# Stick-breaking heads of a two-block model: the order of ScalarE's work, of two projections and of a product

## The reference, cut to what matters

```python
hn = rms_norm(h, norm1_g[i])
z = hn @ w_in[i]
qa, ka, va, qb, kb, vb, ob, ib, fb, uc, vc = split_cols(z, IN_SPLITS)
ya = rms_norm(stick_breaking_attention(qa, ka, va), sb_out_g[i])       # 6 heads of 64
qk = jax.nn.silu(causal_depthwise_conv(jnp.concatenate([qb, kb], axis=-1), conv_w[i], conv_b[i]))
hb = mlstm_chunkwise(qb, kb, vb, ib + igate_b[i], fb + fgate_b[i])     # 4 heads of 96
yb = rms_norm(hb, ...) * jax.nn.sigmoid(ob)
yc = rms_norm(spatial_gating(jax.nn.gelu(uc), jax.nn.gelu(vc), ...), sgu_out_g[i])  # 4 groups of 64
h = h + jnp.concatenate([ya, yb, yc], axis=-1) @ w_out[i]
h = h + hierarchical_moe(...)                                          # 32 experts, 2 per token
```

## Time and profile before

| what | value |
|---|---|
| median of 3 runs | 1323.96 us |
| lowest and highest of them | 1319.77, 1328.98 us |
| the profiled execution's own time | 1326.66 us |
| its span, first to last instruction | 1324.9 us |
| mean granted TensorE clock | 0.928 |
| stick-breaking heads in it | 95 to 156 us |
| mLSTM heads and output projection | 156 to 214 us |

### The profile page before, as it was taken

How to read it: one execution, slowest core, us unless ns; L and a number is a source line. 1 busy time by engine, 2 the same in 40 slices (tenths; PEclk the granted TensorE clock), 3 DMA queues, 4 the chain that set the end, 5 groups by cost and what they waited for, 6 DMA issues and landing times.

```text
span 1324.9 us, 21110 instructions
## 1 busy us (share of the span) xinstructions
PE 1147.2 (87%) x7589; PEld 627.8 (47%) x7589; DVE 573.3 (43%) x1638; ACT 244.1 (18%) x510; POOL 34.0 (3%) x174
## 2 busy tenths in 40 slices
PE   6898899995665796999988998997999989979997
PEld 4655555542222345854444445643444534445434
DVE  3552537432222212899775626433233333323334
ACT  2022322110000224001235313111011111111111
POOL 1000100000000000000110001000000000000000
PEclk9898878998778897999999998999899989989989
DMA  9995548689999973354422455679989999999995
GB/s 328 381 343 220 192 155 317 263 346 421 421 420 422 386 240 127 128 190 141 176 90 101 150 193 207 240 302 428 425 335 427 422 414 428 426 414 423 426 406 204
DMA packets 87309, 399.97 MB, mean 302 GB/s; under 512 B 10646, under 2 KB 19352, under 8 KB 58544
## 3 DMA queue, kind: packets, MB, share of 16 engines
q1 hardware_dynamic: 86272, 398.15, 75.8%
q10 hardware_dynamic: 816, 0.52, 0.3%
q0 software_dynamic: 128, 0.03, 0.0%
HBM read 397.60 MB, written 1.07 MB: 301 GB/s over the span
## 4 chain that ended last, share of the span: by engine, by line
PE 46%; DMA 9%; DVE 3%; ACT 1%; SPq 1%; issue 1%; ACTq 1%; DVEq 0%
PE ps L2411 17%; PE ps L468 10%; PE ps L501 7%; DMA big<-in_w_exp_down 7%; PE ps L427 4%; PE ps L440 2%; PE ps L2447 2%; DMA ring<-in_w_exp_gu 2%; SPq L139 1%; SPq L144 1%; PE ps L417 0%; PE ps L487 0%; ACTq L1014 0%; DVE big L2207 0%; DVE big L2205 0%
## 5 line engine op out<-in xcount | busy, mean ns | idle before, releaser
L468 PE MATMUL ps<-ring,big 128*32 128x512 f32 x1936 | 259.1, 615 | 66.7 <-DMA ring<-in_w_up 45.8
L468 PEld LDWEIGHTS ps<-ring,big 128*32 128x32 f32 x1936 | 75.8, 114 | 204.0 <-issue 204.0
L501 PE MATMUL ps<-big 128*32 128x512 f32 x1120 | 140.2, 645 | 35.5 <-DMA big<-in_w_exp_down 28.1
L2411 PE MATMUL ps<-ring,big 128*128 128x512 f32 x320 | 139.7, 599 | 1.4 <-ACTq L1006 0.9
L468 PE MATMUL ps<-big 128*32 128x512 f32 x304 | 121.2, 623 | 0.0
L427 PEld LDWEIGHTS ps<-big 128*128 128x128 bf16 x1776 | 104.4, 98 | 30.0 <-issue 27.7
L427 PE MATMUL ps<-big 128*128 128x128 bf16 x1776 | 113.5, 219 | 1.4 <-ACT big L287 1.4
L2193 DVE SCALAR_TENSOR_TENSOR big<-big 128x256 f32<-128x256 f32 x240 | 105.6, 481 | 9.3 <-issue 0.4
L2411 PEld LDWEIGHTS ps<-ring,big 128*128 128x128 f32 x320 | 61.2, 192 | 78.1 <-issue 76.2
L501 PEld LDWEIGHTS ps<-big 128*32 128x32 f32 x1120 | 37.6, 117 | 110.9 <-issue 108.6
L287 ACT COPY big<-ps 128x512 f32<-128x512 f32 x74 | 43.4, 586 | 181.5 <-PE ps L427 181.5
(11 more groups left out here) (488 smaller groups left out, 1215.0 us busy)
## 6 DMA issues: line engine op xcount, KB each, us to landing
ring<-in_w_exp_gu SPq DMA_DIRECT2D x55, 2048.0 KB, 17.6
big<-in_w_exp_down SPq DMA_DIRECT2D x64, 1024.0 KB, 13.1
big<-in_w_down SPq DMA_DIRECT2D x32, 1024.0 KB, 18.3
ring<-in_w_in SPq DMA_DIRECT2D x15, 2048.0 KB, 9.0
ring<-in_w_gate SPq DMA_DIRECT2D x28, 1024.0 KB, 18.0
ring<-in_w_up SPq DMA_DIRECT2D x28, 1024.0 KB, 20.0
ring<-in_w_ada SPq DMA_DIRECT2D x12, 2048.0 KB, 16.6
big<-in_w_exp_gu SPq DMA_DIRECT2D x9, 2048.0 KB, 18.6
```

The lines of the kernel that those rows point to most:

```text
L468: last = pe.matmul(ps[rows, BG, :], m.xsT[:, k, rows], m.gu(gu[j], k), start=(k == 0), stop=(k == KC - 1), skip_group_check=True)
L501: last = pe.matmul(ps[rows, BD + n, :], m.hidT[:, k, rows], m.dring[:, down[j], k * D + n * 512:k * D + n * 512 + 512], start=(k == 0), st ...
L2411: last = pe.matmul(bank, lhs(k), rhs(k), start=(k == 0 and start), stop=(k == kk - 1))
```

## The change

Four edits. (1) `W_IN` names block 2304 before block 1920, so the later projections 0 and 1 are the output gate and 2 and 3 the values; the evacuations are swapped with them. (2) On ScalarE the three functions of the next head (`sb_log(h + 1)`) are issued right behind this head's weights, ahead of `conv_silu()` and of the evacuation. (3) VectorE's sigmoid of the output gate becomes `output_gate(t)`, one tile each at the end of heads 3 and 4; the step between mLSTM heads 1 and 2 goes. (4) The mixing is four products of 128 columns (two tiles of 64 side by side), 8 instructions.

```diff
@@
-                (1920, 384, 20, 0), (2304, 384, 22, 4))
+                (2304, 384, 20, 0), (1920, 384, 22, 4))
@@ later_projection(i) of ScalarE
                     if i < TT:
+                        take(ob[:, t, :], lambda b: b[:, 0:MLW], ACT.Exp, scale=-1.0)
+                    else:
                         take(vba[:, t, :, 0:MLD], lambda b: b[:, 0:MLW].rearrange("p (h d) -> p h d", h=MLH))
-                    else:
-                        take(ob[:, t, :], lambda b: b[:, 0:MLW], ACT.Exp, scale=-1.0)
@@ ScalarE, head loop
-                for h in range(SBH):
-                    zb = ps[:, 4 + h % 2, 0:3 * P]
+
+                def sb_log(h):
+
                     act.wait_ge(ev("sb_z"), h + 1)
                     if h >= 2:
                         act.wait_ge(ev("sb_softplus"), h - 1)
-                    act.activation(spt[:, h % 2, :], zb, ACT.Abs)
+                    act.activation(spt[:, h % 2, :], ps[:, 4 + h % 2, 0:3 * P], ACT.Abs)
                     act.drain()
                     act.activation(spt[:, h % 2, :], spt[:, h % 2, :], ACT.Exp, scale=-1.0)
                     act.drain()
                     act.activation(spt[:, h % 2, :], spt[:, h % 2, :], ACT.Ln, bias=1.0).then_inc(ev("sb_ln"), 1)
+                sb_log(0)
+                for h in range(SBH):
                     act.wait_ge(ev("sb_r"), h + 1)
                     if h >= 2:
                         act.wait_ge(ev("sb_y"), h - 1)
-                    act.activation(amt[:, h % 2, :], zb, ACT.Exp).then_inc(ev("sb_weights"), 1)
+                    act.activation(amt[:, h % 2, :], ps[:, 4 + h % 2, 0:3 * P], ACT.Exp).then_inc(ev("sb_weights"), 1)
+                    if h + 1 < SBH:
+                        sb_log(h + 1)
                     if h == 4:
                         conv_silu()
                     for i, half in LATER_HALVES[h]:
@@ VectorE
+                def output_gate(t):
+
+                    dve.wait_ge(ev("proj_evac"), 18 + t + 1)
+                    dve.tensor_scalar(ob[:, t, :], ob[:, t, :], 1.0, None, ALU.add)
+                    dve.drain()
+                    dve.reciprocal(ob[:, t, :], ob[:, t, :])
@@ end of VectorE's head loop
+                    if h >= 3 and h - 3 < TT:
+                        output_gate(h - 3)
@@ VectorE, behind mLSTM head 1
                         dve.drain().then_inc(ev("ya_ready"), 1)
-                        dve.wait_ge(ev("proj_all"), 1)
-                        dve.tensor_scalar(ob, ob, 1.0, None, ALU.add)
-                        dve.drain()
-                        dve.reciprocal(ob, ob)
@@ TensorE, the mixing
-                for t in range(TT):
-                    for gg in range(SGG):
-                        c = t * SGW + gg * SGD
-                        last = pe.matmul(ps[:, 2, c:c + SGD], sgwT[:, gg, :], uv[:, t, 1, gg * SGD:(gg + 1) * SGD],
-                                         start=True, stop=True)
+                for gg in range(SGG):
+                    o = slice(gg * SGD, (gg + 1) * SGD)
+                    last = pe.matmul(ps[:, 2, :].rearrange("p (t c) -> p t c", t=TT)[:, :, o], sgwT[:, gg, :], uv[:, :, 1, o],
+                                     start=True, stop=True)
```

## The result

The changed kernel takes 1314.82 us (median of 8 runs, 1311.68 to 1319.83), the kernel before 1325.33 us (8 runs, 1319.77 to 1332.2): a ratio of 0.9923, 95% interval 0.9904 to 0.9943. By the ratio that is 10.2 us less, with 7.6 to 12.7 us by the interval (the medians differ by 10.5); 14.2 were forecast. The share of 0.8% lies in "the same" by the bound of 1%, to which the forecast gave 0.45, against 0.51 for "faster". The profiled execution took 1314.38 us and has a span of 1312.5 us; the kernel before had one of 1324.9.

What follows compares the result with a forecast made beforehand. TensorE, busy 87% of the span, was taken as the bound, with waits for GpSimd's mask and low-clock stretches. Terms 8.26 + 4.2 + 1.7 = 14.2 us off 1326.66 gave 1312.5 us; range 1303 to 1319.5 us.

Steps and rivals of the forecast that it cites:

- the bound of 1%: Whole kernel: a measurement tells about 1%, 13.2 us, so a time counts as faster only under 1310.7 us.
- The waits of `sb_r`, 8.26 us: Stick-breaking heads: TensorE's four waits for GpSimd's mask all go, 1.75 + 3.05 + 1.75 + 1.71 = 8.26 us.
- The clock in the heads, 4.2 us: Head loop: with the waits gone TensorE stays at 2.4 GHz, saving 2.56 + 1.64 = 4.2 us.
- `conv_silu` behind head 5's Ln, 0.7 us to spare: Head 4 on ScalarE: `conv_silu` and the evacuation still end before head 5's weights are due, with 0.7 us spare.
- The loads of sgu_w: Issued at about 135.5 us, the last lands at 141.3, before first use near 143.3; a slip costs up to 1 us.
- Edits 1 and 3, nothing: Output gate: swapping blocks costs nothing, the split gate hides on VectorE, and removing its 5.5 us behind mLSTM head 1 gains nothing.
- The mixing, 1.7 us: Mixing on TensorE: half the instructions at equal spacing save 8 x 0.215 = 1.7 us; bounds nothing to 1.7.
- I pass the sum on whole: Behind the changed part: the whole 14.2 us gained by `y_ready` reaches the kernel's end, as later loads follow the products.
- the signs of being wrong: `sb_r` waits for softplus behind the reciprocal; late sgu_w loads; clock falls in the loop; 14 us missing after the first experts.
- the rivals: Chances: costlier low clock 0.15, clock stays up 0.06, mixing saves nothing 0.05, loads absorb it 0.08, clock turns it round 0.04.
- the costlier low clock in the mLSTM stretch: Between head loop and mixing: 4.6 us of work at half speed; gain only 10.5 us, 1313.5 us; chance 0.15.

Runs made afterwards that it cites:

- edit 4: Only the mixing in four products of 128 columns, against the kernel before: ratio 1.0013 (0.9996 to 1.0031).
- both of these padded: The kernel before, and the one with only the new mixing, each plus four idle TensorE products: ratios 1.0029 and 1.0007 to the kernel before.
- the kernel with the gate late: The changed kernel with edits 1 and 3 undone, one add and reciprocal of 768 columns behind mLSTM head 1: 1316.31 us, ratio 0.9906 to the kernel before.
- the padded kernel: The changed kernel plus four idle TensorE products ahead of its wait for the first rows: ratios 0.9908 and 0.9901 (1311.94 us) to the kernel before.
- edit 2 alone: Only ScalarE's new order, with blocks, gate and mixing as before, against the kernel before: 1316.65 us, ratio 0.9923.
- the kernel before, padded: The kernel before plus four idle TensorE products ahead of its wait for the first rows: ratio 1.0029 (1.0016 to 1.0042) to the kernel before.

## Why the prediction was right or wrong

- *The waits of `sb_r`, 8.26 us:* right. All five later heads run at TensorE's own pace.
- *The clock in the heads, 4.2 us:* right. Heads 1 to 4 take 30.5 us in every trace with edit 2, and 41.5 to 42.4 in the four without it (before; edit 4; both of these padded): 11 to 12 us less from head 1's `sb_r` to head 5's, where 8.26 - 1.75 + 4.2 = 10.7 follow from the forecast. Head 1's own wait comes on top.
- *`conv_silu` behind head 5's Ln, 0.7 us to spare:* right in kind, 0.4 us in size; ScalarE was idle 0.38 us before head 5's weights.
- *The loads of sgu_w:* the bound "up to 1 us" was reached, 1.12 us in the first trace (0.68 and none in the two others of the same kernel), and I had left it out of the sum. I took the old 5.8 us to landing. The issues moved to 135.1 to 136.1 us, and SP's load of w_out goes out at 136.04; before the change they went out at 144.2 to 145.2 and w_out at about 146.8, when the last of them had a lead of 1.6 us. The view of DMA issues after the change:

```profile
ring<-in_w_out SPq DMA_DIRECT2D x1, 2048.0 KB, 11.0
big<-in_sgu_w ACTq DMA_DIRECT2D x1, 256.0 KB, 2.9
big<-in_sgu_ln_g ACTq DMA_DIRECT2D x1, 128.0 KB, 5.5
big<-in_sgu_ln_b ACTq DMA_DIRECT2D x1, 128.0 KB, 8.5
```

  The row sgu_ln_b took 7.2 to 8.7 us to land in the seven traces in which it went out within 0.1 us of w_out, 5.8 with a lead of 1.6 us, and 4.5 and 4.7 with a lead of 8: the small rows share the engines with the 2 MB. When two streams are moved, their distance is a term too.
- *Edits 1 and 3, nothing:* right, by the trace of the kernel with the gate late; its times tell no more than some 2 us.
- *The mixing, 1.7 us:* right in place (8 instructions, 1.6 to 1.7 us less). By the rule of the Trainium skill ("TensorE: Matmul & The Clock Gate", "Part 2: What happens when you issue a matmul") it would have been nothing, as the prediction says. Here the measurement decides: at the low clock 16 instructions of 64 columns took 3.44 us from start to start, 8 of 128 columns 1.84, so 0.215 and 0.23 us each. In the times of edit 4 the gain doesn't show, padded or not.
- *"I pass the sum on whole":* this step failed; 3.2 us of the 15.6 were lost at the exit from the first rounds. The loads did follow, as argued: from `y_ready` to the last round the trace keeps its lead (15.6 us, then 15.3 at the rounds near 380 us, and 15.6 at the last). What I hadn't priced was the length of TensorE's code. By the padded kernel against the changed one this is worth 2.7 us (standard error 1.0). Of the signs of being wrong that the prediction names, two came: the late loads, and the gain at `y_ready` that isn't all there at the end of the first experts.

The sum with what the first trace shows: 14.2 - 1.1 (the load) - 3.2 (the first exit) - 0.8 (the second block's first products, cause open) + 1.2 (the last exit) = 10.3 us, against 10.2 measured (7.6 to 12.7). That it comes out so near is luck in part: the wait for the load was smaller in the other two traces, the mixing's 1.7 us haven't shown by themselves in the times, and the clock's own changes from run to run are as large as these terms. The range held the time; the likeliest value didn't hold the size.

None of the rivals names the loss. The first, the costlier low clock in the mLSTM stretch, gave almost the right number, but occurred only in part and not always: from the transposes of sgu_w to the mixing it took 5.15 us before, and 7.35, 4.93 and 5.14 in the three traces of the changed kernel. Behind the mixing the clock went the other way: 12.7 us from the mixing to the transposes in the traces where it came back in the middle, 15.7 where it didn't.

## What to carry to other kernels

Before a stage is credited with what an edit saves in it, look for places behind it where the engine waits for "issue" at the exit of a loop, and see in the DMA view whether a packet of code lies in front of them or in them: here 16 instructions more or fewer ahead of them moved such a wait by 1.5 us or more, with the low clock behind it, which is more than edit 4 gave. An "idle" control that lengthens the code is then no control; compare layouts, too. And in a chain over four engines, issue the next item's work before the evacuation that has to wait for the longest one: edit 2 alone, without a single instruction more, brought as much as the whole change (10.2 us each, within some 3 us).

## What the runs showed of the hardware that was not expected

- At the exit from the first block's rounds TensorE starts its next product 2.6 us after the start of a 16 KB packet of the instruction queue, in all 13 traces. It sits idle for 1.0 to 1.3 us where the packet starts with the last products, and for 2.5 to 2.7 us where it starts as they end. In these five traces, and in no other, the clock is at 1.2 GHz behind the wait (3.2 to 3.3 us for the eight products of line 440 in place of 2.1). At the last exit of the kernel before, padded, the wait was 3.47 us, again with the low clock behind it (3.75 us for the eight products).
- Runs of one kernel differ by up to 12 us (the kernel before, 8 runs). The traces show one source in the changed part: the length of head 0 with the clock's state there (from the first `sb_z` to the second `sb_r` the changed kernel takes 14.54, 11.58 and 11.53 us in its three traces). Another lies in the second block's rounds, where traces drift apart by up to 3 us and mostly come together again; between 1254 and 1278 us (of the kernel before) the lead over the kernel before changes by -0.9 to +2.4 us for good.
- A reciprocal of 384 columns takes VectorE 2.56 us, one of 768 columns 4.95.
